# A two-block transformer on one core: the end of the first block reordered, its low part given whole to GpSimd

## The reference, cut to what matters

```python
# end of the first block
    h = h + jnp.einsum('bsf,fd->bsd', jax.nn.silu(gate) * val, w_down[l])
return rmsnorm(h, norm_final_g)
...
# start of the second block; rms_norm(x, g) = x * rsqrt(mean(x*x) + 1e-6) * g
for layer in range(2):
    y = rms_norm(h, norm_mix[layer])
    y = hgrn2_mixer(...) if layer == 0 else moba_mixer(...)   # begins with y @ w_in
    h = h + y
    h = h + swiglu(rms_norm(h, norm_ffn[layer]), ffn_w13[layer], ffn_w2[layer])
return rms_norm(h, final_norm)
```

## Time and profile before

| what | us |
|---|---|
| three runs | 984.64, 985.51, 985.61 (median 985.51) |
| the profiled execution, its own time | 984.77 |
| its span, first to last instruction | 982.9 |
| around the span | 1.87 |
| PE busy | 973.6 |
| DVE, ACT, POOL busy | 675.0, 543.0, 43.7 |

### The profile page before, as it was taken

The page is one execution under the profiler, slowest core; times in us unless marked ns, Lnnn a source line. Parts: engine busy times, 40 slices in busy tenths (PEclk is TensorE's granted clock), DMA queues, the critical chain, the costliest instruction groups (busy, mean ns, idle before and its releaser), DMA issues.

```text
span 982.9 us, 15510 instructions
## 1 busy us (share of the span) xinstructions
PE 973.6 (99%) x6230; PEld 841.1 (86%) x6230; DVE 675.0 (69%) x908; ACT 543.0 (55%) x719; POOL 43.7 (4%) x68
## 2 busy tenths in 40 slices
PE   9999999999999999999999999999999999999997
PEld 8888878988888889888898888888888898888886
DVE  6688877698787789678576555556656565646465
ACT  6787664576555666535455545454555555444453
POOL 2210000000000005000000000000000000000000
PEclk9999999999999999999999999999999999999999
DMA  9363346466655536743447565656553545656541
GB/s 291 124 222 121 117 152 210 162 208 211 206 178 198 187 128 219 228 159 131 150 147 248 163 218 180 217 176 214 182 175 136 174 149 192 214 171 212 172 171 44
DMA packets 121443, 175.88 MB, mean 179 GB/s; under 512 B 3199, under 2 KB 89802, under 8 KB 121386
## 3 DMA queue, kind: packets, MB, share of 16 engines
q1 hardware_dynamic: 119020, 168.82, 51.7%
q0 software_dynamic: 1600, 5.09, 1.8%
q10 hardware_dynamic: 766, 1.16, 0.5%
HBM read 173.82 MB, written 1.25 MB: 178 GB/s over the span
## 4 chain that ended last, share of the span: by engine, by line
PE 98%; DVE 1%; ACT 1%; issue 0%; POOL 0%; POOLq 0%; DVEq 0%
PE ps L1993 27%; PE ps L2035 23%; PE ps L2043 12%; PE ps L2021 12%; PE ps L2067 4%; PE ps L2590 3%; PE ps L2075 2%; PE ps L2593 2%; PE ps L2123 1%; PE ps L2532 1%; PE ps L2314 1%; PE ps L2360 1%; PE ps L2603 1%; PE ps L2351 1%; PE ps L2448 1%; PE ps L2465 1%
## 5 line engine op out<-in xcount | busy, mean ns | idle before, releaser
L1149 DVE TENSOR_TENSOR w_lo<-raw,w_hi 128x2048 fp32r<-128x2048 f32 (+3 forms) x159 | 360.5, 2271 | 98.0 <-ACT w_hi L554 97.4
L554 ACT ACTIVATE w_hi<-raw 128x2048 fp32r<-128x2048 f32 (+1 forms) x159 | 298.8, 1881 | 66.9 <-PE ps L1993 46.1
L2035 PE MATMUL ps<-x_both,w_hi 128*128 128x512 f32 x992 | 232.9, 390 | 0.0
L2035 PEld LDWEIGHTS ps<-x_both,w_hi 128*128 128x128 f32 x992 | 184.8, 188 | 37.4
L2043 PEld LDWEIGHTS ps<-x_both,w_lo 128*128 128x128 f32 x992 | 125.1, 191 | 3.6
L2043 PE MATMUL ps<-x_both,w_lo 128*128 128x256 f32 x992 | 126.2, 283 | 0.0
L839 ACT ACTIVATE work<-ps 128x512 f32<-128x512 f32 x66 | 39.2, 593 | 149.1 <-PE ps L2043 133.9
L1582 DVE TENSOR_TENSOR work<-ps,work 128x512 f32<-128x512 f32 x66 | 45.4, 688 | 81.2 <-ACT work L839 80.9
L1993 PE MATMUL ps<-w_hi,x_both 128*128 128x512 f32 (+1 forms) x320 | 99.9, 386 | 0.0
L1993 PE MATMUL ps<-w_hi,hid_hi 128*128 128x512 f32 (+1 forms) x242 | 94.3, 390 | 0.0
L1993 PE MATMUL ps<-w_lo,hid_hi 128*128 128x512 f32 (+1 forms) x242 | 94.1, 389 | 0.0
(11 more groups left out here) (301 smaller groups left out, 1150.1 us busy)
## 6 DMA issues: line engine op xcount, KB each, us to landing
raw<-in_ffn_w SPq DMA_DIRECT2D x66, 1024.0 KB, 5.2
raw<-in_w_up SPq DMA_DIRECT2D x22, 1024.0 KB, 5.1
raw<-in_hgrn_w_in SPq DMA_DIRECT2D x16, 1024.0 KB, 5.4
raw<-in_w_in SPq DMA_DIRECT2D x12, 1024.0 KB, 5.2
raw<-in_moba_w_in SPq DMA_DIRECT2D x12, 1024.0 KB, 5.1
raw<-in_w_down SPq DMA_DIRECT2D x11, 1024.0 KB, 4.9
raw<-in_w_out SPq DMA_DIRECT2D x4, 1024.0 KB, 6.1
raw<-in_hgrn_w_out SPq DMA_DIRECT2D x4, 1024.0 KB, 5.2
```

The source lines that it names most:

```text
L554: act.activation(w_hi[:, n % RING, 0:kc * cols], raw[:, n % RING, 0:kc * cols], ACT.Copy).then_inc(s["hi_ready"], 1)
L1149: dve.tensor_tensor(w_lo[:, n % RING, sl], raw[:, n % RING, sl], f32(w_hi[:, n % RING, sl]), ALU.subtract).then_inc(s["lo_ready"], 1)
L2035: pe.matmul(out, w_hi[:, n % RING, 256 * k + P * f:256 * k + P * f + P], x_both[:, k, :, :], start=(k == 0), stop=False)
```

## The change

It makes five edits. (1) In the first network `last_down_high_first` takes all six products of half 0 first and then all six of half 1. (2) POOL makes the whole low part of granule nf in one instruction of 2048 columns; DVE's half is gone, and so is POOL's wait for the scaled row: what is left of its waits is met long before. (3) The gain and the squares of a half follow directly on its addition, and the sums go to a tile `sums` of five columns (the fifth is 1), so that a variance is one multiply-and-sum of five (or three) numbers with fixed shares. (4) At the same border the turns move two places later in the third granule's products, the turns of tile 0 stand after the 6th and the 8th of the last 12 down matmuls instead of after the 10th and the 12th, and ACT writes both pieces of nf+2 after all squares of tile 1. (5) At the third network ACT writes the third granule's high part in two pieces, and PE takes it so; its turns of tile 1 stand after the fourth and the eighth matmul instead of after the second and the sixth.

```diff
@@ setup of the vector engine
+            for t in range(TT):
+                dve.memset(sums[:, t, 4:5], 1.0)
+            dve.memset(shares[:, 0, 0:2], 1.0 / D)
+            for q, (other, rest) in enumerate(((EPS / D, EPS * EPS), (1.0 / D, EPS))):
+                dve.memset(shares[:, q, 2:4], other)
+                dve.memset(shares[:, q, 4:5], rest)
@@ gpsimd, after power() of tile 0
-                    pool.wait_ge(s["row_ready"], step(3, 0, 1))
                     pool.wait_ge(s["hi_ready"], n + 1)
                     pool.wait_ge(s["lo_ready"], n)
-                    pool.wait_ge(s["low_half"], 1)
-                    sl = slice(0, GW // 2)
-                    pool.tensor_tensor(w_lo[:, n % RING, sl], raw[:, n % RING, sl], f32(w_hi[:, n % RING, sl]), ALU.subtract).then_inc(s["lo_ready"], 1)
+                    pool.tensor_tensor(w_lo[:, n % RING, :], raw[:, n % RING, :], f32(w_hi[:, n % RING, :]), ALU.subtract).then_inc(s["lo_ready"], 1)
@@ scalar, border()
-                if k != 6:
+                if k == 7:
+                    for half in range(2):
+                        hi_by_feature(n + 2, half)
+                elif k != 6:
                     hi(n + 2)
@@ scalar, end of the first block
             for c in range(2):
                 square(2, 0, c)
-            for c in range(2):
                 square_scaled(0, c)
             hi(nf + 1)
...
             square(2, 1, 0)
-            hi_by_feature(nf + 2, 0)
+            square_scaled(1, 0)
             square(2, 1, 1)
-            square_scaled(1, 0)
-            hi_by_feature(nf + 2, 1)
+            for half in range(2):
+                hi_by_feature(nf + 2, half)
@@ vector, end of the first block
-            def first_variance(t):
-                v, q = slice(4 + t, 5 + t), slice(6 + t, 7 + t)
-                dve.wait_ge(s["half_ready"], 3 + 2 * t)
-                dve.tensor_scalar(var_half[:, v], ssq_half[:, v], 1.0 / D, EPS, ALU.mult, ALU.add)
-                then(dve.tensor_scalar(var_half[:, q], ssq_half[:, v], EPS / D, EPS * EPS, ALU.mult, ALU.add))
             def both_variances(t):
-                v, q = slice(4 + t, 5 + t), slice(6 + t, 7 + t)
                 dve.wait_ge(s["ssq_ready"], 5 + 2 * t)
-                then(dve.scalar_tensor_tensor(var_half[:, q], ssq[:, v], EPS / D, var_half[:, q], ALU.mult, ALU.add))
                 dve.wait_ge(s["half_ready"], 4 + 2 * t)
-                then(dve.scalar_tensor_tensor(var_half[:, q], ssq_half[:, q], 1.0 / D, var_half[:, q], ALU.mult, ALU.add))
                 dve.wait_ge(s["ssq_ready"], 6 + 2 * t)
-                dve.scalar_tensor_tensor(var[:, q], ssq[:, q], 1.0 / D, var_half[:, q], ALU.mult, ALU.add).then_inc(s["var_ready"], 1)
-                dve.scalar_tensor_tensor(var[:, v], ssq[:, v], 1.0 / D, var_half[:, v], ALU.mult, ALU.add).then_inc(s["var_ready"], 1)
+                for q, col, first in ((0, 6 + t, 0), (1, 4 + t, 2)):
+                    dve.tensor_tensor_reduce(terms[:, t, q, first:5], sums[:, t, first:5], shares[:, q, first:5], 1.0, 0.0,
+                                             ALU.mult, ALU.add, accum_out=var[:, col:col + 1]).then_inc(s["var_ready"], 1)
-            dve.wait_ge(s["hi_ready"], nf + 1)
-            dve.tensor_tensor(w_lo[:, nf % RING, GW // 2:GW], raw[:, nf % RING, GW // 2:GW], f32(w_hi[:, nf % RING, GW // 2:GW]),
-                              ALU.subtract).then_inc(s["low_half"], 1)
             dve.wait_ge(s["final_in"], 16)
-            add_row(0, 0)
-            add_row(0, 1)
-            by_final_gain(0)
-            first_variance(0)
+            for c in range(2):
+                add_row(0, c)
+                by_final_gain(0, c)
             both_variances(0)
             scale_both(0)
             add_row(1, 0)
             operand_lo(3, 0, 0)
+            by_final_gain(1, 0)
             operand_lo(3, 0, 1)
             add_row(1, 1)
-            first_variance(1)
-            by_final_gain(1)
+            by_final_gain(1, 1)
@@ tensor, last_down_high_first
-                    for x, w in ((hid_hi, w_hi), (hid_hi, w_lo), (hid_lo, w_hi)):
+                    order = [(c, x, w) for c in range(2) for x, w in ((hid_hi, w_hi), (hid_hi, w_lo), (hid_lo, w_hi))]
+                    if f != 0:
+                        order.sort(key=lambda term: (term[1] is hid_lo, term[2] is w_lo))
@@ tensor, end of ffn() for f == 0
-                    down_tile(10, n0 + 32, 1, signals=(1,), between={(3, 1): [(k_turn + 1, 0, 0)]})
-                    turn_half(k_turn + 1, 0, 1)
+                    down_tile(10, n0 + 32, 1, signals=(1,), between={2: [(k_turn + 1, 0, 0)], (2, 2): [(k_turn + 1, 0, 1)]})
@@ tensor, the two stages by feature
-                stage_by_feature(n0, k_turn, free=20 if f == 2 else None, turns=((0, 2), (0, 6)) if f == 2 else None)
+                stage_by_feature(n0, k_turn, free=20 if f == 2 else None, turns=((0, 4), (1, 0)) if f == 2 else None, halves=2 if f == 2 else 0)
-            stage_by_feature(nf, 3, turns=((1, 0), (1, 4)), halves=True)
+            stage_by_feature(nf, 3, turns=((1, 2), (1, 6)), halves=1)
```

More of the change, by code:

```diff
@@ L300, in build @@
         ang = sb("ang", [P, 4, TT * 24])
+        sums = sb("sums", [P, TT, 5])
+        shares = sb("shares", [P, 2, 5])
+        terms = sb("terms", [P, TT, 2, 5])
         pos_i = sb("pos_i", [P, TT], I32)
@@ L577, in square @@
                 col = 2 * m + t
-                acc = (ssq if c else ssq_half)[:, col:col + 1]
+                acc = sums[:, t, 2 + c:3 + c] if m == 2 else (ssq if c else ssq_half)[:, col:col + 1]
                 act.activation(xn[:, t, half_row(c)], h[:, t, half_row(c)], ACT.Square, accum_out=acc).then_inc(
@@ L808, in _, with hi_by_feature @@
             f0 = G["ffn0"]
+            def hi_by_feature(n, f):
+                act.wait_ge(raw_in[n % RING], 16 * (n // RING + 1))
+                act.wait_ge(s["products_done"], n - RING + 1)
+                src = raw[:, n % RING, :].rearrange("p (k n) -> p k n", k=DC)[:, :, P * f:P * f + P]
+                dst = w_hi[:, n % RING, :].rearrange("p (k n) -> p k n", k=DC)[:, :, P * f:P * f + P]
+                act.activation(dst, src, ACT.Copy).then_inc(s["hi_ready" if f else "hi_half"], 1)
             def border(k, m, n):
@@ L936, in square_scaled @@
                 act.wait_ge(s["scaled_done"], 2 * t + c + 1)
-                acc = (ssq if c else ssq_half)[:, 6 + t:7 + t]
+                acc = sums[:, t, c:c + 1]
                 act.activation(squared[:, t, half_row(c)], scaled[:, t, half_row(c)], ACT.Square, accum_out=acc).then_inc(
                     s["ssq_ready" if c else "half_ready"], 1)
[L941 to L947, removed]
             hi(nf)
@@ L1682, in add_row, with by_final_gain @@
                 add(t, c, 4 + 2 * c + t)
[L1684 to L1687, removed]
-            def first_variance(t):
-                v, q = slice(4 + t, 5 + t), slice(6 + t, 7 + t)
-                dve.wait_ge(s["half_ready"], 3 + 2 * t)
-                dve.tensor_scalar(var_half[:, v], ssq_half[:, v], 1.0 / D, EPS, ALU.mult, ALU.add)
-                then(dve.tensor_scalar(var_half[:, q], ssq_half[:, v], EPS / D, EPS * EPS, ALU.mult, ALU.add))
+            def by_final_gain(t, c):
+                dve.wait_ge(s["h_added"], 5 + 2 * t + c)
+                dve.tensor_tensor(scaled[:, t, half_row(c)], h[:, t, half_row(c)], g_final[:, half_row(c)], ALU.mult).then_inc(s["scaled_done"], 1)
             def both_variances(t):
-                v, q = slice(4 + t, 5 + t), slice(6 + t, 7 + t)
                 dve.wait_ge(s["ssq_ready"], 5 + 2 * t)
-                then(dve.scalar_tensor_tensor(var_half[:, q], ssq[:, v], EPS / D, var_half[:, q], ALU.mult, ALU.add))
                 dve.wait_ge(s["half_ready"], 4 + 2 * t)
-                then(dve.scalar_tensor_tensor(var_half[:, q], ssq_half[:, q], 1.0 / D, var_half[:, q], ALU.mult, ALU.add))
                 dve.wait_ge(s["ssq_ready"], 6 + 2 * t)
-                dve.scalar_tensor_tensor(var[:, q], ssq[:, q], 1.0 / D, var_half[:, q], ALU.mult, ALU.add).then_inc(s["var_ready"], 1)
-                dve.scalar_tensor_tensor(var[:, v], ssq[:, v], 1.0 / D, var_half[:, v], ALU.mult, ALU.add).then_inc(s["var_ready"], 1)
+                for q, col, first in ((0, 6 + t, 0), (1, 4 + t, 2)):
+                    dve.tensor_tensor_reduce(terms[:, t, q, first:5], sums[:, t, first:5], shares[:, q, first:5], 1.0, 0.0,
+                                             ALU.mult, ALU.add, accum_out=var[:, col:col + 1]).then_inc(s["var_ready"], 1)
             def scale_both(t):
@@ L1731, in _ @@
             dve.tensor_tensor_reduce(squared[:, 1, 512:D], scaled[:, 1, 512:D], scaled[:, 1, 512:D], 1.0, 0.0, ALU.mult, ALU.add,
-                                     accum_out=ssq[:, 7:8]).then_inc(s["ssq_ready"], 1)
+                                     accum_out=sums[:, 1, 1:2]).then_inc(s["ssq_ready"], 1)
             both_variances(1)
@@ L2049, in feature_both, with feature_high @@
```

(19 more changed lines are left out.)

2 lines of the change are left out of this document (1 added, 1 removed).

## The result

The changed kernel takes 989.97 us as the median of five runs (989.04 to 990.41), the kernel before 985.27 us (984.64 to 985.61, five runs): 4.7 us more, ratio 1.0046, 95% interval 1.0036 to 1.0057 (the three runs above are among these five). It is slower by half a per cent, as forecast; 989.2 us was predicted, in a range of 986.0 to 991.5. The profiled execution took 990.41 us, with a span of 988.8 against 982.9.

What follows compares the result with a forecast made beforehand. PE, busy almost throughout, was taken to bound the kernel. Border +3.5, clock +1.4 and third network -0.5 gave +4.4 us on the profiled 984.77: 989.2 us, range 986.0 to 991.5.

Steps and rivals of the forecast that it cites:

- What can be won: PE's waits at the second block's border and the third network's entry: the five edits win back at most 2.3 us.
- Edit 1: Last down product by halves: the fifth matmul waits for `hid_lo`, PE slips 0.19 us, DVE's first addition starts earlier.
- The chain: Gain, squares and variance at the border: sum of five taken at 0.2 us, POOL's power 0.45 us earlier.
- POOL's duration: POOL's whole low part of 2048 columns: 4.57 us by the trace's slope, with a sign of 4.6 to 5.4 us.
- Who holds the port: POOL's low part against tile 0's L1710: one holds the port for its whole instruction; one L1710 takes 4.5 to 5.3 us.
- The border without the clock: Border to the second block: the held port makes tile 1's turn late, +3.5 us, PE's 0.19 us slip included.
- The clock: PE's gap of about 4.4 us at the border may lower the granted clock: 1.4 us taken, bounds nothing and 5.8.
- The third network: Third network's entry: PE's wait for ACT's high part goes whole, -0.5 us.
- The sum: Whole kernel: 3.5 + 1.4 - 0.5 = +4.4 us, 989.2 us on the profiled execution's 984.77.
- The rival without the clock (B, 987.8): At the border the port is held but the clock does not fall: +3.0 us, 987.8; chance 0.30.
- Rival C: Both L1710 go before POOL, whose port hold then delays `by_final_gain(1, 0)`: +2.3 - 0.5, about 986.8 us; chance 0.10.
- Rival D: At the border POOL's subtract runs in small steps and lets DVE in between: 983.7 to 984.4 us; chance 0.15.

Runs made afterwards that it cites:

- best kernel here: The changed kernel with edit 2 undone and the gain of tile 1's half 0 moved back behind tile 0's second low half: 984.21 us, ratio 0.9989.
- the kernel with the filled gap: The changed kernel with 18 unused matmuls of 512 columns in PE's gap before the first turn of tile 0: 988.10 us, ratio 1.0028.
- POOL's half beside the gain: The changed kernel with edit 2 undone, so the low part is split between DVE and POOL as before: 984.74 us, ratio 0.9993.
- POOL waits: The changed kernel with POOL's old wait for `row_ready` put back ahead of the whole low part: 988.00 us, ratio 1.0027.
- in pieces: The changed kernel with POOL's low part in eight instructions of 256 columns instead of one: 984.82 us, ratio 0.9997.
- edit 2 alone: The kernel before with only edit 2, POOL making the whole low part without the wait for the scaled row: 990.24 us, ratio 1.0051.

## Why the prediction was right, step by step

**What can be won.** 2.3 us was the ceiling. The best kernel here won 1.1 of it by the medians; its profile shows 0.4 at the border (its shift) and 0.56 at the third network, and the 0.1 between is within the scatter.

**Edit 1.** Predicted slip 0.19 us; the twelve matmuls took 362.15 - 359.20 = 2.95 us in place of 2.72 (358.64 to 361.36), 0.23. The prediction had all of it in the wait for `hid_lo`; the profile has two waits of PEld, 0.3 us for `hid_lo` and 0.2 for `w_lo`, and the second was not foreseen. DVE's first addition came 1.58 us after `hid_lo` started, where it was 2.28: 0.70 earlier, predicted 0.71.

**The chain.** Power predicted 0.45 us earlier; from `hid_lo` it is 364.97 - 359.46 = 5.51 us against 364.81 - 358.90 = 5.91: 0.40 earlier. The sum of five was taken at 0.2 us and is 0.17 with its read by 364.88.

**POOL's duration.** 4.57 us by the trace's slope, 4.51 measured, and 4.60 in the kernel with the filled gap. 4.51 lies just under the 4.6 to 5.4 that the prediction gave as its sign. The Trainium skill's page "GPSIMD Engine Reference", section "Instruction dispatch", gave an estimate of 4.27 us; the measurement lies 0.24 over that.

**Who holds the port.** The first L1710 was predicted at 4.5 to 5.3 us if it lost, and it took 5.01. POOL was first, by 0.05 us, and DVE's real start, 5.01 - 0.75 = 4.26 us after its recorded one, lies at 369.8, 0.2 us before POOL's end. The rule of the Trainium skill's "SBUF — State Buffer", section "Who interferes with whom", by which one of the two holds the port for a whole instruction, agrees with every kernel here: 5.01 us (changed), 1.71 (POOL's half beside the gain), 3.88 (POOL waits) and 1.22 (in pieces).

**The border without the clock.** Predicted +3.5 us; the filled kernel shows +3.62. PE's gap was predicted at about 4.4 us; it is 4.23 for PE (366.40 to 370.63) and 4.65 for PEld.

**The clock.** This is the term that was mis-sized: I took 1.4 us, half of a low stretch of 2.8, on the guess that it lasts as long as it took to fall. The runs show 1.9 us in the medians and 2.25 in the profiled pair. In the profile the low stretch lasts from 369.2 to 376.0, 6.8 us, and PE works through its last 5.4 of them, which is 2.7 us of lost work, of which 2.25 show in the shift; where the other 0.4 went was not traced. The fall itself came 2.8 us after the last matmul, as at the kernel's end. The bounds, 0 and 5.8 us, held it. That the clock falls at all had a chance of 0.40 against 0.30, so the total's closeness owes something to luck.

**The third network.** Predicted -0.5 us, measured -0.56, alone or with the rest, and -0.65 in the medians when alone.

**The sum.** +4.4 predicted, +4.7 in the medians, +5.9 in the spans, of which 0.56 is the late start. The parts as measured, 3.6 + 1.9 - 0.6 = 4.9 us, lie further from the forecast than the medians do. From the median of before, 985.27, the same +4.4 would give 989.7, against 989.97; 989.2 rests on the lower 984.77. The rival without the clock (B, 987.8) is what the filled kernel is (988.1). Rival C's mechanism, the hold falling on `by_final_gain(1, 0)`, is what the kernel with the restored wait shows: +2.45 against the +2.3 worked out. (C's time was put at 986.8; its +1.8 in all gives 986.6 on the profiled execution and 987.3 on the median.) Rival D would have needed pieces, and with pieces it nearly comes: 984.8, not the 984.1 in the middle of D's range. Each L1710 still loses 0.47 us, and two instructions of tile 1's chain lose 0.28 and 0.27, for which the turn of tile 1 then waits.

## What to carry to other kernels

In these kernels work given to GpSimd and the DVE instructions with two SBUF inputs that fell beside it held each other up, whichever came second, while those with one operand in PSUM kept their 0.69 us. Before moving such work, list DVE's instructions with two SBUF inputs in the time that it will take, and look at which of them the tensor engine waits for. If they must overlap, try GpSimd's work in pieces no longer than the delay that you can bear: here eight pieces cost GpSimd 3.4 us and saved the kernel about 5. A wait that seems idle, like the one for `row_ready`, can be what keeps two engines apart, but only as long as the work behind it ends before DVE's next such instruction: with the whole low part behind it, it only moved the hold. And a gap of the tensor engine like those here, 3.2 and 4.7 us, is to be priced with the clock that it may lose, not only with its own length.

## What I had not expected of the hardware

The clock stayed low for 6.8 us in the profile of the changed kernel and for only some 3.4 in that of the kernel with edit 2 alone. There PE came back at 371.13, still at full speed, and the clock fell only at about 372.5, as the windows show: the granted clock was 0.50 (1.2 GHz) to 375.9.

```profile
372.00:372.50 0.50, 0.50 (x6) 0.36 (x4) 0.39 (x2) 0.42 (x1) 0.00 (x0) 0.97 0.76 129
372.50:373.00 0.50, 0.27 (x2) 0.00 (x0) 0.50 (x1) 0.19 (x1) 0.00 (x0) 0.50 0.86 258
375.50:376.00 0.50, 0.50 (x5) 0.50 (x4) 0.50 (x2) 0.46 (x2) 0.00 (x0) 0.62 0.00 0
```

So two gaps of the same cause and nearly the same length (4.7 and 4.4 us) cost 5.87 and 4.62 us of shift; the two kernels differ in the other four edits too, so not all of that difference need be the clock's. What decides when after a gap the clock falls, and how long it stays low, these runs don't settle. Whether it differs between executions of one kernel was looked at only by the mean clock, and there the 3.2 us stop is the other surprise: six of nine executions had the lower one.
